# Two transformer blocks on one core: where a duo's transposes and products stand in the attention's beats

## The reference

```
x = x + gated_mix(attention_A(h), attention_B(h), attention_C(h)) @ w_out     # block 1, then an MLP
for l in 0, 1:                                                               # block 2
    x = x + swiglu(h);  x = x + gated_mix(attention_a2(h), pool(h), attention_c2(h)) @ w_out;  x = x + swiglu(h)
```

## Time and profile before

| | |
|---|---|
| three runs | 3504.93, 3510.7, 3511.44 us (median 3510.7) |
| the profiled execution | 3509.4 us |
| its span, first to last instruction | 3507.6 us |
| TensorE busy in it | 3407.7 us, 97% |
| mean granted TensorE clock | 0.992 of full speed |

### The profile page before, as it was taken

One profiled execution on the slowest core, in us unless ns is written; L12 is line 12 of the kernel. 1 busy time (PEld: TensorE's weight loads), 2 busy tenths in 40 slices (PEclk: granted clock), 3 DMA queues, 4 the chain that ended last, 5 costly groups with the idle time before them and its releaser, 6 DMA issues.

```text
span 3507.6 us, 42466 instructions
## 1 busy us (share of the span) xinstructions
PE 3407.7 (97%) x17034; PEld 2738.9 (78%) x17034; DVE 1186.1 (34%) x2514; ACT 883.3 (25%) x1876; POOL 2370.5 (68%) x1242
## 2 busy tenths in 40 slices
PE   8978999999999999999999999999999999999999
PEld 6655777988898888667779888888887677798887
DVE  6554342433443234552223111332245422241111
ACT  2656552211120002354312000210012543221000
POOL 7514547787778776645677877687775546678775
PEclk9999999999999999999999999999999999999999
DMA  3212223344535442212232222254432222223232
GB/s 142 68 60 82 73 64 102 143 175 168 187 132 198 175 165 94 73 58 82 85 103 102 96 97 95 80 218 167 170 129 73 67 75 79 82 97 103 98 100 73
DMA packets 104771, 388.08 MB, mean 111 GB/s; under 512 B 12016, under 2 KB 12400, under 8 KB 98432
## 3 DMA queue, kind: packets, MB, share of 16 engines
q1 hardware_dynamic: 88272, 292.76, 25.3%
q10 hardware_dynamic: 16304, 92.62, 6.9%
HBM read 383.20 MB, written 2.13 MB: 110 GB/s over the span
## 4 chain that ended last, share of the span: by engine, by line
PE 91%; DVE 4%; ACT 4%; issue 1%; ACTq 0%; DVEq 0%
PE psum L1202 28%; PE psum L1204 27%; PE psum L1203 27%; PE psum L1275 2%; PE psum L1317 2%; PE psum L1292 2%; PE psum L1261 1%; DVE rs_t L1663 1%; DVE s_sb L1704 1%; ACT s_sb L1445 0%; ACT s_sb L1463 0%; ACT L1445 0%; ACT L1415 0%; PE psum L1253 0%; ACT rs_t L1415 0%
## 5 line engine op out<-in xcount | busy, mean ns | idle before, releaser
L1170 POOL TENSOR_TENSOR w_hi<-raw,ones 128x1024 fp32r<-128x1024 f32 (+2 forms) x593 | 1041.3, 1756 | 981.0 <-PE psum L1204 973.1
L1173 POOL TENSOR_TENSOR w_lo<-raw,w_hi 128x1024 fp32r<-128x1024 f32 (+2 forms) x593 | 1316.4, 2220 | 46.5
L1202 PE MATMUL psum<-h_hi,w_hi 128*128 128x512 f32 (+2 forms) x2912 | 1141.9, 392 | 30.5 <-DVE r L1679 20.5
L1204 PE MATMUL psum<-h_hi,w_lo 128*128 128x512 f32 (+2 forms) x2912 | 1106.2, 380 | 0.0
L1203 PE MATMUL psum<-h_lo,w_hi 128*128 128x512 f32 (+2 forms) x2912 | 1105.6, 380 | 0.0
L1202 PEld LDWEIGHTS psum<-h_hi,w_hi 128*128 128x128 f32 (+1 forms) x2912 | 550.3, 189 | 167.4 <-issue 33.9
L1204 PEld LDWEIGHTS psum<-h_hi,w_lo 128*128 128x128 f32 (+1 forms) x2912 | 550.1, 189 | 106.7
L1203 PEld LDWEIGHTS psum<-h_lo,w_hi 128*128 128x128 f32 (+1 forms) x2912 | 551.0, 189 | 101.0 <-issue 7.2
L1202 PE MATMUL psum<-a_hi,w_hi 128*128 128x512 f32 (+1 forms) x1064 | 392.5, 369 | 0.0
L1203 PE MATMUL psum<-a_lo,w_hi 128*128 128x512 f32 (+1 forms) x1064 | 391.9, 368 | 0.0
L1204 PE MATMUL psum<-a_hi,w_lo 128*128 128x512 f32 (+1 forms) x1064 | 391.8, 368 | 0.0
(11 more groups left out here) (198 smaller groups left out, 3305.0 us busy)
## 6 DMA issues: line engine op xcount, KB each, us to landing
raw<-weights_dram SPq DMA_DIRECT2D x487, 512.0 KB, 3.4
ada_t<-ada_dram ACTq DMA_DIRECT2D x48, 1536.0 KB, 7.1
raw<-weights_dram SPq DMA_DIRECT2D x76, 256.0 KB, 2.7
raw<-weights_dram SPq DMA_DIRECT2D x32, 384.0 KB, 3.1
bias_t<-biases_dram ACTq DMA_DIRECT2D x36, 256.0 KB, 2.9
bias_t<-cum_dram ACTq DMA_DIRECT2D x16, 256.0 KB, 4.1
out_dram<-x SPq DMA_DIRECT2D x8, 256.0 KB, 2.0
raw<-weights_dram SPq DMA_DIRECT2D x4, 408.0 KB, 3.2
```

The costliest lines, as they stand in the source:

```text
L1170: nc.gpsimd.tensor_tensor(high, piece, ones[:, 0:1].to_broadcast([P, n]), ALU.mult)\
L1173: nc.gpsimd.tensor_tensor(w_lo[:, p % NR, 0:n], piece, high.bitcast(F32), ALU.subtract)\
L1202: mm(dst, lh, rh, start=first, stop=False)
L1204: return mm(dst, ll, rh, start=False, stop=last)
```

## The change

All attentions get the same four beats, and `turns` and `copy` take duo j instead of duo j+1.

```diff
     def turns(j):
-        if 0 <= j + 1 < n:
-            u = duos[j + 1]
+        if 0 <= j < n:
+            u = duos[j]
...
     def copy(j):
-        if 0 <= j + 1 < n:
-            put("copy", duos[j + 1])
+        if 0 <= j < n:
+            put("copy", duos[j])
...
-        if kind == "att_a":
-            out += [(lambda j=j: scores(j), w), (lambda j=j: (exps(j), turns(j)), w),
-                    (lambda j=j: (products(j), copy(j), scale(j)), 2 * w)]
-        elif kind in ("att_b", "att_c", "att_c2"):
-            out += [(lambda j=j: (scores(j), products(j)), w), (lambda j=j: (exps(j), low(j)), w),
-                    (lambda j=j: (turns(j), copy(j)), w), (lambda j=j: scale(j), w)]
-        else:
-            out += [(lambda j=j: scores(j), w), (lambda j=j: (exps(j), turns(j)), w),
-                    (lambda j=j: (products(j), copy(j)), w), (lambda j=j: (low(j), scale(j)), w)]
+
+        out += [(lambda j=j: (turns(j), scores(j), copy(j)), w), (lambda j=j: exps(j), w),
+                (lambda j=j: products(j), w), (lambda j=j: (low(j), scale(j)), w)]
```

## The result

| | before | after |
|---|---|---|
| four runs each, median (range) | 3511.07 us (3504.93 to 3512.27) | 3548.68 us (3547.54 to 3551.57) |
| ratio, 95% interval | | 1.0113 (1.0097 to 1.0129) |
| span of the profiled execution | 3507.6 us | 3545.7 us |

The forecast was 3510.3 in a range of 3501 to 3521; the measured time is 38 us above it and outside. After the change the same work stands six lines earlier in the code: L1275 is L1269, L1292 is L1286, L1304 and L1317 are L1298 and L1311, L1478 is L1472, L1734 is L1728, L1704 is L1698.

A forecast was written before the change was run, and what follows sets the result against it. PE, busy in 97% of the span, was taken as the bound. Terms -1.1 (att_a), +0.5 (att_b), +1.9 (att_c), -1.7 (att_a2) gave -0.4 on 3509.4, or 3509.0; with 1.3 for the median, 3510.3 us, range 3501 to 3521.

The forecast's parts named there:

- A bias DMA now has a copy in front of it in ACT's queue: All attentions: a copy of 0.4 to 1.0 us precedes the bias DMA, whose tile is used a pair later.
- Sum +1.9, bounds 0 to +5: att_c: nine iterations without dense chunks wait 0.33 us each, +3.0; a low part +0.4; today's product waits go.
- +0.5, bounds -9 to +4: att_b: high and low parts before the scaling +3.9, ACT's waits absorb 2.3, a transposes' wait of 1.1 us goes.
- -1.7, bounds -3 to +1: Both att_a2: in the first, transposes' waits of 1.45 and 0.5 us go and 0.3 returns; in the second these cancel.
- `att_c2`, 0: Both att_c2: no change, as a dense chunk pair stands in every beat pair that matters.
- `att_a`, -1.1, bounds -5 to +8.1: att_a: duo 4 0.0, duo 7 -1.7, duos 9 to 11 +0.5, duos 12 to 14 -1.6, duo 15 +1.7 us.
- the scaling of duo 15: att_a: root steps in front make score 16 come 3.0 us later; 1.3 comes back, so +1.7.
- the terms of duos 12 to 14 and 15: att_a: duos 12 to 14 gain 1.6 us as copies leave the way; duo 15 loses 1.7.
- Scaling paid in full: Rival, att_a: root steps in front of the scaling delay each next score; +8.1 instead of -1.1, 3519.5 us; chance 0.13.
- The waits did not go outright: Rival: half of 15.7 us of transposes' and products' waits and two half-rate stretches go; -14, 3496 us; chance 0.15.
- Half rate did spread: Rival: longer waits before three att_a scores each bring a new half-rate stretch of 3.2 us; +9.6, 3520 us; chance 0.07.
- the three scores that I had named: att_a: scores 10, 11 and 16, whose waits of 2 to 4 us could each bring a half-rate stretch.

The follow-up runs named there:

- e8: Kernel after with copy in front of scores and bias load and products one beat later, plus scores in front of transposes in att_c alone; 3510.20 us, 0.9999.
- e1: Kernel after with the copy in front of the scores and so of the bias load in ACT's queue, all attentions; 3527.54 us, 1.0047.
- e4: Kernel after with the copy in front of scores and bias load, and the products one beat later, in all attentions; 3514.40 us, 1.0013.
- e2: Kernel after with the beat reordered to scores, transposes, copy, bias load in all attentions; 3535.64 us, 1.0074.
- e7: Kernel before with only att_a changed, and there only the scaling moved one beat back; 3513.45 us, 1.0009.
- e10: Kernel before with the bias load moved from behind the scores to directly in front of the copy (in att_a, att_a2 the products), two beats later; 3505.46 us, 0.9985.

## Why the prediction was wrong, step by step

The loss against before, in three steps by the ratios: the copy behind the bias load 23 us (1.0113 to 1.0047), the products' place 12 (to 1.0013), transposes in front of scores in `att_c` 5 (to 0.9999). The intervals leave each step uncertain by 5 to 8 us. Of the second step `att_c`, where products were too close behind their copy, has 4.0; the two `att_a2` have 11.3, by the pool's step, and part of that is offset elsewhere. That e8 ends at 0.9999 does not mean that nothing is left: its `att_c` is still 5.2 and each `att_c2` 3.3 us longer than before, and a shorter `att_a` stands against it.

- **"A bias DMA now has a copy in front of it in ACT's queue": this step failed.** It is the other way round: the copy has the bias DMA in front of it. I read the three calls of the beat as three steps and did not follow `scores` into `load_bias`. The prediction took such a DMA for a mere transfer, "its tile is used a pair later", and did not ask what its issue waits for. This error is the largest, and it stood in no bound, so the range could not hold the time. The Trainium skill has the rule: page "DMA: Bandwidth & Descriptors", section "Anatomy of one DMA — SWDGE (gpsimd) path", says that DMA engines do not wait on semaphores, and that any such wait is made by the sequencer that issues. That section is on DMAs of another engine, but the trace agrees for those of ACT: ACT stood 2.16 us before 442.50, with the load's wait and its issue of 0.82 in it.
- **"Sum +1.9, bounds 0 to +5" for `att_c`.** Measured +20.1. Of this 7.9 is the bias load (after less e1), half-rate stretches behind its waits included. The narrow distance that I priced, 0.33 us for each of nine small iterations, is 5.3 us of waits in e1, tail included, and e4 gave 4.0 back: the mechanism was right, at some twice the price. A part as large was not seen at all: the transposes' own time on PE went from 17.9 to 25.3 us in e1. I had said that PE's work between two scores stays the same; its amount does, its duration doesn't.
- **`att_b`, "+0.5, bounds -9 to +4".** Measured +8.7, or +5.2 from duo 17's scores on; e1 takes back 4.2 and e4 another 5.2. ACT has no slack there, and a copy behind a bias load delays everything behind it; products then wait in front of the scores. Products' waits for copies there rose from 8.9 to 13.4 us in the kernel after and are 9.8 in e1 and 9.7 in e4; so e4's shorter `att_b` is not these waits, and 4 us of it may be chance.
- **`att_a2`, "-1.7, bounds -3 to +1".** The transposes' wait did go, as forecast. But the stage took 7.0 and 7.8 us more: 2.4 of each is the bias load, the rest went when the products moved (e4). I held that the products kept 1.4 us of dense work behind their copy. That is true and was not the point. No term had the other queues' timing in it: the wait for the pool's step, 4.0 us with DVE beside POOL, and 3.4 us of half rate behind it.
- **`att_c2`, 0.** Measured +2.1 and +2.2, unchanged by e1. In the first of them the transposes' own time on PE, start to start, went from 7.4 to 9.8 us, and in e2, where scores stand in front, it is 7.5. So the price found in `att_c` is paid here too; but e2's stage is only 0.7 shorter, since its dense work and scores take 1.6 more.
- **`att_a`, -1.1, bounds -5 to +8.1.** Measured -6.9 at the last L1734, outside the bounds, but -3.4 at the first scores of `att_b`, within them. Counting L1704's starts in the profiles, duo by duo, the gain grows from duo 7 to duo 8 by 2.4 (forecast 1.7), by another 1.2 to duo 9 (in no term), falls from duo 9 to 12 by 0.5 (forecast 0.5), grows from duo 12 to 15 by 2.9 (forecast 1.6), and falls from there to duo 17 by 3.0 (forecast 1.7). The last is the scaling of duo 15: the score behind it waits 3.88 us where it waited 1.22, 2.7 more (forecast 3.0), and the 1.3 that was to come back did not. So the mechanism held duo by duo, and the terms of duos 12 to 14 and 15 were mis-sized most, one against the other. Duo 7's root end, which the earlier trace rows show at 150.38 with PE waiting for it, now comes in front of the scaling (DVE, kernel after):

```profile
146.03 0.69 DVE L1670 TENSOR_TENSOR br_a<-psum,br_a 128x512 fp32r<-128x512 f32 x1 [0.66 <-ACT br_a L1539]
...
147.77 0.75 DVE L1728 SCALAR_TENSOR_TENSOR s_sb<-psum,row_scale,s_sb 128x512 f32<-128x512 f32 x1 [0.92 <-ACT row_scale L1451]
```

- **The rivals.** Scaling paid in full fell: e7 has it alone, and it costs at most 0.2%. The waits did not go outright. Half rate did spread, but for the most part elsewhere: of the three scores that I had named one got such a stretch (score 16, granted clock 0.57 from 214 to 218 us), while the clock in `att_a` as a whole rose, from 0.94 to 0.96. The new ones stand in `att_c` behind a wait for a copy and in both `att_a2` behind the pool's step. The rule on transposes from the Trainium skill, "TensorE: Matmul & The Clock Gate", "Part 4: PE-mode transpose", would have made the place of the transposes the cause of new half-rate stretches. The runs show no such effect: `att_a` has 0.96 in e1, with transposes in front of the waiting scores, and 0.93 in e2, with scores in front. That does not test the rule itself, since dense work stands around both. No rival had the bias load, so all chances were put on the wrong list. Of the signs named in advance, that of being wrong (a stage moves by more than 7) came true in `att_c`; the one for the scores of `att_a` (waits for L1734 up from 15.0) hardly moved, to 16.2.

## What to carry to other kernels

When a step moves within a queue, write out that engine's queue after the change, with what each instruction waits for, DMA issues among them; a load that nobody needs soon still blocks all behind it while it waits. A distance in beats is worth what stands in these beats, so look at the iterations where they are empty. Small matmuls can cost more in front of other small ones than in front of dense work: count the time from start to start beside each possible neighbour in the trace before moving one. And choose the mark at which a stage ends on the engine that sets the pace; a mark on another engine can move by itself.

## What the runs showed that I had not expected

- The same transposes on PE take longer or shorter by what follows them: from start to start 0.13 us (two of 31 columns) in front of dense matmuls and 0.31 in front of scores; six of 128 columns 0.63 and 0.75. Scores cost the same in front of transposes and of dense work (0.63). What in the engine makes the difference no run here shows.
- A single wait of PE of 1.86 us was followed by 4 us at a mean granted clock of 0.57, while the stage ran at 1.00 from 340 us up to it and from 447 to 560. Here so short a wait cost about as much again (0.43 of 4 us, 1.7 us).
- Two DVE instructions that take 0.42 and 0.69 us alone took 2.00 and 2.71 when POOL's splits of a weight tile had begun before them, and each ended only behind POOL's. POOL's own took 1.89 and 2.39 us, against 1.89 and 2.41 before.
- The issue of two loads takes ACT's queue 0.82 us. Between a wait and the instruction that ends it this is paid; beside a running ACTIVATE it is hidden (e10).
